# Chunk 0's value products moved from the start of its attention to its projection units, with its rows' affine passes

## What is computed

```
x    = layer_norm(x, emb_ln_g, emb_ln_b)
proj = x @ w_in          # u_pool 512 | q 512 | c 128 | iq 512 | ik 64 | iw 8
pool_out = per-group matmul of (trailing-window mean of u_pool - u_pool), windows 2,4,8,16
c    = rms_norm(c)       # the shared key/value latent
o    = sparse attention: scores from iq, ik, iw; causal top 256; softmax over c with bias
attn = o @ w_uv
x    = layer_norm(ALPHA*x + concat(pool_out, attn) @ w_o)
x    = layer_norm(ALPHA*x + square(relu(x @ w_up)) @ w_down)
```

## Time and profile before

| | |
|---|---|
| median of 3 runs | 1262.57 us (1261.06 to 1264.2) |
| the profiled execution, its own time | 1262.74 us |
| its span in the profile | 1261.0 us |
| PE busy | 1196.6 us (95%) |
| DVE, ACT, POOL busy | 867.2, 540.3, 518.0 us |
| mean granted TensorE clock | 0.987 |

### The profile page before, as it was taken

One profiled execution on the slowest core, in us unless ns is written; L12 is line 12 of the kernel. 1 busy time (PEld: TensorE's weight loads), 2 busy tenths in 40 slices (PEclk: granted clock), 3 DMA queues, 4 the chain that ended last, 5 costly groups with the idle time before them and its releaser, 6 DMA issues.

```text
span 1261.0 us, 16226 instructions
## 1 busy us (share of the span) xinstructions
PE 1196.6 (95%) x5551; PEld 962.9 (76%) x5551; DVE 867.2 (69%) x1291; ACT 540.3 (43%) x875; POOL 518.0 (41%) x396
## 2 busy tenths in 40 slices
PE   5999997789989999999999999979899999999997
PEld 4776785567888878778778768868788888888886
DVE  6388989686957888898998878867534233243357
ACT  4545542565246334334234266652342442433440
POOL 2235788433435676676676653212102102103002
PEclk9999899899999999999999999999999999999999
DMA  7723431101303233233333210035122333323331
GB/s 221 251 75 109 142 100 51 67 2 34 101 27 124 84 117 110 91 116 100 99 103 114 62 56 1 2 134 134 66 100 86 109 97 95 116 85 98 116 101 67
DMA packets 126852, 118.63 MB, mean 94 GB/s; under 512 B 5773, under 2 KB 99530, under 8 KB 126794
## 3 DMA queue, kind: packets, MB, share of 16 engines
q1 hardware_dynamic: 126794, 117.86, 30.4%
HBM read 107.34 MB, written 10.50 MB: 93 GB/s over the span
## 4 chain that ended last, share of the span: by engine, by line
PE 76%; DVE 9%; POOL 7%; issue 3%; ACT 2%; DMA 2%; POOLq 0%; DVEq 0%; SPq 0%; ACTq 0%
PE g_bank L1641 14%; PE g_bank L1642 14%; PE g_bank L1643 14%; PE wide L1641 8%; PE wide L1643 8%; PE wide L1642 8%; PE g_bank L1799 3%; POOL wlo L453 3%; PE g_bank L1601 2%; POOL rows L858 1%; DVE win L628 1%; PE wide L1758 1%; PE wide L1705 1%; PE wide L1706 1%; POOL rstd L779 1%
## 5 line engine op out<-in xcount | busy, mean ns | idle before, releaser
L453 POOL TENSOR_TENSOR wlo<-wring,whi 128x1024 fp32r<-128x1024 f32 (+1 forms) x94 | 229.8, 2446 | 204.4 <-ACT whi L1505 123.4
L1641 PE MATMUL g_bank<-xhi,whi 128*128 128x512 f32 (+2 forms) x768 | 301.4, 392 | 4.3 <-DVE xlo L694 3.9
L1642 PE MATMUL g_bank<-xlo,whi 128*128 128x512 f32 (+2 forms) x768 | 297.7, 388 | 0.0
L1643 PE MATMUL g_bank<-xhi,wlo 128*128 128x512 f32 (+2 forms) x768 | 297.6, 388 | 0.0
L1505 ACT ACTIVATE whi<-wring 128x1024 fp32r<-128x1024 f32 x120 | 127.1, 1059 | 355.9 <-PE wide L1643 179.8
L453 DVE TENSOR_TENSOR wlo<-wring,whi 128x1024 fp32r<-128x1024 f32 (+1 forms) x66 | 84.4, 1278 | 197.8 <-ACT whi L1505 192.8
L1641 PE MATMUL wide<-whi,hhi 128*128 128x512 f32 x480 | 190.2, 396 | 0.7 <-POOL wlo L453 0.7
L1643 PE MATMUL wide<-whi,hlo 128*128 128x512 f32 x480 | 189.6, 395 | 0.0
L1642 PE MATMUL wide<-wlo,hhi 128*128 128x512 f32 x480 | 189.6, 395 | 0.0
L1641 PEld LDWEIGHTS g_bank<-xhi,whi 128*128 128x128 f32 (+1 forms) x768 | 144.6, 188 | 39.7 <-DVE xlo L694 4.3
L1643 PEld LDWEIGHTS g_bank<-xhi,wlo 128*128 128x128 f32 (+1 forms) x768 | 144.6, 188 | 33.0 <-issue 0.6
(11 more groups left out here) (238 smaller groups left out, 1953.4 us busy)
## 6 DMA issues: line engine op xcount, KB each, us to landing
wring<-in_w_up SPq DMA_DIRECT2D x64, 512.0 KB, 4.1
wring<-in_w_down SPq DMA_DIRECT2D x64, 512.0 KB, 3.7
wring<-in_w_in SPq DMA_DIRECT2D x26, 512.0 KB, 3.9
wring<-in_w_o SPq DMA_DIRECT2D x16, 512.0 KB, 4.1
rows<-in_x SPq DMA_DIRECT2D x8, 512.0 KB, 4.9
normalized_rows<-rows SPq DMA_DIRECT2D x8, 512.0 KB, 6.9
rows<-normalized_rows SPq DMA_DIRECT2D x4, 512.0 KB, 5.1
emb_stage<-normalized_rows SPq DMA_DIRECT2D x4, 512.0 KB, 4.6
```

The costliest lines, as they stand in the source:

```text
L453: eng.tensor_tensor(parts_of(name, lo_tile(name)), parts_of(name, wring[n % 4]), parts_of(name, hi_tile(name)).bitcast(F32), ALU.subtract) ...
L1641: nc.tensor.matmul(out_ap, w_hi, m_hi, start=first, stop=False)
L1642: nc.tensor.matmul(out_ap, w_hi, m_lo, start=False, stop=False)
L1643: return nc.tensor.matmul(out_ap, w_lo, m_hi, start=False, stop=last)
```

## The change

Chunk 0's values are formed among its own projection units: `("vv", 0, k)` enters the order of `tokens_queries(0)`, PE and ACT form it there, and DVE's low parts go into its loop over n. The latents of chunk 0 are rounded right after they are made, into tiles of their own (`latT0_hi`, `latT0_lo`), and their low part is made before the poolings. Values 2 and 3 use the tiles at 104.25 and 108.25 KB, where `gains` lies; so ACT waits before each value for the four blocks of `emb_gains`, and SP waits for the last value product of the attention (`pv_full`, 16) before it loads the next gains. `emb_gains` now works on the rows before they are spilled: POOL starts it once iq unit 1 is split, and does its eight passes, the latents' inverse (`latents_inverse_rms`) and the subtraction for `wuv_lo` among its first splits. The rows that come back from the spill area need nothing more. `head_masks` waits for unit q3 of chunk 1 and no longer for po3.

```diff
-    order = ("u0 u1 u2 po0 u3 po1 q0 po2 q1 po3 q2 q3", "q0 q1 q2 u0 u1 u2 po0 u3 po1 q3 po2 po3")[c]
+    order = ("u0 u1 vv0 u2 vv1 po0 u3 vv2 po1 q0 vv3 po2 q1 po3 q2 q3", "q0 q1 q2 u0 u1 u2 po0 u3 po1 q3 po2 po3")[c]
...
-        names += [("vv", c, k) for k in ((0, 1, 2, 3), (2, 3, 4, 5, 6, 7))[c]]
+        names += [("vv", 1, k) for k in range(2, NB)] if c else []
...
+LAST_UNIT = ("q", 1, 3)
...
+        latT0_hi = part("latT0_hi", 84.25, [P, CHUNK], F32R)
+        latT0_lo = part("latT0_lo", 86.25, [P, CHUNK], F32R)
...
+            tile = v_part[k] if c == 0 and k >= 2 else v_tiles[k]
...
-            load_units(units[4:7])
-
+            load_units(units[4:8])
+
+            sp.wait_ge(bias_row_ready, 1)
+            sp.dma_start(bias_rows, bias_row[:, :]).then_inc(bias_out, 16)
             for b in range(CB):
-                sp.wait_ge(xhat_ready, b + 1)
+                load_units(units[8 + b:9 + b])
+                if b == 1:
+                    sp.wait_ge(bias_out, 16)
+                    sp.wait_ge(wuv_lo_ready, 1)
+                    sp.dma_start(near_up[:, :, :], ...).then_inc(bias_in, 16)
+                sp.wait_ge(emb_rows, b + 1)
                 sp.dma_start(spilld[b], rows[:, b, :]).then_inc(spilled, 16)
             sp.wait_ge(spilled, 16 * CB)
-
-            sp.wait_ge(g_full, EV[("xT", 0, KT - 1)])
             for b in range(CB):
                 sp.dma_start(rows[:, b, :], xd[CB + b]).then_inc(x_in[CB + b], 16)
-
-            sp.wait_ge(bias_row_ready, 1)
-            ...
-            load_units(units[7:U[("iq", 1, 3)]])
+            load_units(units[12:U[("iq", 1, 3)]])
...
-            sp.wait_ge(emb_rows, CB)
+            sp.wait_ge(pv_full, 16)
             load_gains(ln1_g, ln1_b)
...
-                pool.wait_ge(g_full, EV[("po", 1, 3)])
+                pool.wait_ge(g_full, EV[LAST_UNIT])
...
-            def emb_gains():
+            def emb_gains(b):
 
                 pool.wait_ge(gains_in, 32)
-                for b in range(CB):
-                    pool.wait_ge(rows_in, 16 * (b + 1))
-                    ...
+                pool.wait_ge(g_full, EV[("xT", 0, KT - 1)])
+                link(pool.tensor_tensor(rows[:, b, :], rows[:, b, :], gains[:, 0, :], ALU.mult))
+                pool.tensor_tensor(rows[:, b, :], rows[:, b, :], gains[:, 1, :], ALU.add).then_inc(emb_rows, 1)
...
             inverse_std(EMB0)
+
+            pool.wait_ge(*LO[("iq", 0, 1)])
+            emb_gains(0)
+            emb_gains(1)
+            latents_inverse_rms(0)
             pool.wait_ge(wuv_hi_ready, 1)
             pool.tensor_tensor(wuv_lo[:, :], wuv_raw[:, :], wuv_hi[:, :].bitcast(F32), ALU.subtract).then_inc(wuv_lo_ready, 1)
-            latents_inverse_rms(0)
-            lo(*units[U[("u", 0, 0)]:U[("q", 0, 2)]])
+            emb_gains(2)
+            lo(("u", 0, 0))
+            emb_gains(3)
+            lo(*units[U[("u", 0, 0)] + 1:U[("q", 0, 2)]])
...
-            gained = emb_gains()
-            for name in units[U[("iq", 1, 3)] + 3:U[("wo", 0, 0, 2)]]:
-                lo(name)
-                next(gained)
+            lo(*units[U[("iq", 1, 3)] + 3:U[("wo", 0, 0, 2)]])
             head_masks(0)
...
             keys_queries_lo(dve, 0, chain, lambda p: split_lo(dve, dve_lo[3 + p], lo_dve) if p < 3 else None)
+            latents_lo(0)
...
                 add_score(2 * n + 1)
+                if 1 <= n <= 4:
+                    values_lo(0, n - 1)
...
-            latents_lo(0)
             attention(0)
...
                 copy_out(("cT", c), latT[:, c * CHUNK:(c + 1) * CHUNK], bank(("cT", c))[:, :], scale=kv_g)
+                if c == 0:
+                    act.wait_ge(g_evac, EV[("cT", 0)])
+                    nc.scalar.activation(latT0_hi[:, :], latT[:, 0:CHUNK], ACT.Copy).then_inc(latT_hi_ready, 1)
...
+                    if name[0] == "vv":
+                        act.wait_ge(emb_rows, CB)
+                        values_hi(0, n)
+                        continue
...
-            act.wait_ge(iq_lo_ready, 2 * CB)
-            nc.scalar.activation(latT_hi[:, 0:CHUNK], latT[:, 0:CHUNK], ACT.Copy).then_inc(latT_hi_ready, 1)
             attention(0)
...
+                    if name[0] == "vv":
+                        values(0, name[2])
+                        continue
...
-                for k in ((0, 1, 2, 3), (2, 3, 4, 5, 6, 7))[c]:
-                    values(c, k)
+                for k in range(2, NB) if c else ():
+                    values(1, k)
```

More of the change, by code:

```diff
@@ L270, in layer, with v_pairs @@
         v_tiles = v_keep + v_part + [whi[1]]
-        def v_pairs(k):
-            return v_tiles[k][:, :].rearrange("p (a b d) -> p a b d", a=4, b=4)
+        def v_pairs(c, k):
+            tile = v_part[k] if c == 0 and k >= 2 else v_tiles[k]
+            return tile[:, :].rearrange("p (a b d) -> p a b d", a=4, b=4)
         def halves(v):
@@ L388, in layer @@
             units += [("ik", c), ("c", c)] + [("iq", c, p) for p in range(4)]
-            units += [name for name in tokens_queries(c) if name[0] != "po"]
+            units += [name for name in tokens_queries(c) if name[0] in ("u", "q")]
         for c in range(2):
@@ L832, in head_masks @@
                 spread_reciprocals(8 * c + 7)
-            def emb_gains():
+            def emb_gains(b):
                 pool.wait_ge(gains_in, 32)
-                for b in range(CB):
-                    pool.wait_ge(rows_in, 16 * (b + 1))
-                    link(pool.tensor_tensor(rows[:, b, :], rows[:, b, :], gains[:, 0, :], ALU.mult))
-                    yield b
-                    pool.tensor_tensor(rows[:, b, :], rows[:, b, :], gains[:, 1, :], ALU.add).then_inc(emb_rows, 1)
-                    yield b
+                pool.wait_ge(g_full, EV[("xT", 0, KT - 1)])
+                link(pool.tensor_tensor(rows[:, b, :], rows[:, b, :], gains[:, 0, :], ALU.mult))
+                pool.tensor_tensor(rows[:, b, :], rows[:, b, :], gains[:, 1, :], ALU.add).then_inc(emb_rows, 1)
             def staged_gains(b):
@@ L1080, in latents_lo @@
                 at = slice(0, CHUNK * (c + 1))
+                hi_part, lo_part = ((latT0_hi, latT0_lo), (latT_hi, latT_lo))[c]
                 dve.wait_ge(latT_hi_ready, c + 1)
-                nc.vector.tensor_tensor(latT_lo[:, at], latT[:, at], latT_hi[:, at].bitcast(F32), ALU.subtract)\
+                nc.vector.tensor_tensor(lo_part[:, :], latT[:, at], hi_part[:, :].bitcast(F32), ALU.subtract)\
                     .then_inc(latT_lo_ready, 1)
@@ L1126, in attention @@
                         mask_logits(step)
-                    if step == 32 * c:
-                        for k in ((0, 1, 2, 3), (2, 3, 4, 5, 6, 7))[c]:
-                            values_lo(c, k)
+                    if c and step == 32:
+                        for k in range(2, NB):
+                            values_lo(1, k)
                     if 32 * c + 2 <= step < 32 * c + 34:
@@ L1165, in add_residual @@
                 dve.wait_ge(rows_in, 16 * CB * (c + 1))
-                dve.wait_ge(emb_rows, CB * (c + 1))
+                if c:
+                    dve.wait_ge(emb_rows, 2 * CB)
                 for nh, u, b in projection_steps():
@@ L1423, in attention @@
                 exps(lo)
-                for k in ((0, 1, 2, 3), (2, 3, 4, 5, 6, 7))[c]:
-                    values_hi(c, k)
+                for k in range(2, NB) if c else ():
+                    values_hi(1, k)
                 for step in range(lo, lo + LAST_STEP):
@@ L1742, in values @@
                 free(name)
-                three_passes(bank(name)[:, :], latT_hi[:, at], latT_lo[:, at], wuv_hi[:, :], wuv_lo[:, :], True, True)\
+                three_passes(bank(name)[:, :], hi_part[:, at], lo_part[:, at], wuv_hi[:, :], wuv_lo[:, :], True, True)\
                     .then_inc(g_full, 1)
```

14 lines of the change are left out of this document (6 added, 8 removed).

## The result

The changed kernel takes **1256.14 us** (median of 6 runs, 1253.44 to 1258.6) where the kernel before takes 1262.42 (6 runs beside them, 1261.06 to 1264.2). The ratio is 0.9948 with a 95% interval of 0.9933 to 0.9963: 6.3 us faster. The profiled execution of the changed kernel took 1258.6 us (span 1256.8), 4.1 less than the profiled one of before. It is the slowest of the six; the granted clock of the six is between 0.990 and 0.996, and the two fastest runs, 1253.44 and 1255.12 us, have the highest, 0.996 and 0.995.

A forecast was written before the change was run, and what follows sets the result against it. PE was taken to bind until 113 us, and DVE's poolings, in turns with POOL, from 189.63. -13.4 + 2.8 + 1.1 + 6.4 = -3.1 against 1262.74 gave 1259.6, so 1259.5 us as median; range 1252.5 to 1265.

The forecast's parts named there:

- rival A: Among the iq units, POOL and DVE operations fit each other's gaps, so Part 3 is 0: 1253.1 us; chance 0.22.
- Part 3: Among the iq units, POOL's added passes delay DVE's splits: PE waits 1.3 and 3.5 us, low clock 1.6; loss 6.4 us.
- Part 2: In chunk 0's u and q units, four values cost PE 2.8 us and waits at po1 and po2 1.1.
- `values_lo` would be the releaser: In chunk 0's units, waits before po1 and po2 stay below 1 us and end with `values_lo`.
- Part 1: End of chunk 1's projections and attention's start: earlier poolings and values moved away bring the fourth logits forward; gain 13.4 us.
- Rival D: At the attention's start, masks wait for something other than the last split; about 8 us gained, 1265 us; 0.18 with B.
- 1.2 us for a low clock: At the attention's new start, PE idles between 214.6 and 218 us and the clock falls; 1.2 us (0 to 2.5) given back.
- the wait before po1: End of chunk 1's projections: po1's 0.67 us wait for pooled group 1 goes, moving everything to q3 forward by 0.67.
- The edits costed at nothing: Chunk 0's latent rounding, ACT's wait for `emb_rows`, later spills and loads, and SP's later w_o load have slack; 0 us.
- Rivals B and C: B: DVE falls behind in chunk 0's units, 1261 to 1265 us, 0.18 with D. C: turns continue, 1266.8 us, 0.10.
- the two stretches that I placed: Low clock after PE idles: 1.6 us lost among the iq units and 1.2 us at the attention's new start.

The follow-up runs named there:

- e1: Changed kernel without POOL's eight passes over chunk 0's rows, all waits kept; 1251.86 us, ratio 0.9910 to the kernel before.
- e4: Changed kernel's work in another POOL order, keeping passes clear of DVE's subtractions and splits for iq units 2 and 3; 1251.61 us, ratio 0.9907.
- e5: Changed kernel with each block's two passes replaced by four memsets of the same rows, which read nothing; 1252.2 us (one run).
- e3: Changed kernel with values early, but eight same-size passes back behind POOL's last eight splits of chunk 1; 1260.05 us, ratio 0.9980.
- e6: Changed kernel with POOL's last split before the masks moved into the attention, ahead of mask 18; 1255.07 us, ratio 0.9938.
- e7: e4 with wuv_lo ahead of block 2's passes, these around u0's split, and block 3's passes together behind u1's split; 1257.76 us, ratio 0.9957.
- e2: Changed kernel with passes early, but chunk 0's values and latent rounding put back at the attention's start; 1255.84 us, ratio 0.9943.
- e9: e4 with wuv_lo right behind the first four passes and the last split late as in e6; 1248.9 us, ratio 0.9895.
- e10: e9 with the values late as in e2; 1250.33 us, ratio 0.9908 to the kernel before.

## Why the prediction was right, and where its sizes were off

The time lies in the range, 3.4 us under the predicted 1259.5. The gain is 6.3 us where 3.1 were forecast, and the result is 0.4 us below the forecast's own range (1256.5 to 1262.5), towards rival A, which did not happen. The kernel is faster by more than the noise, an outcome given 0.42 against 0.48 for no change. So the range held in part because it was wide enough for rival A. Each mechanism named was there; what was off is a sum of small terms and the clock.

- **Part 3, the turns among the iq units** (predicted +6.4). The step held: waits of 1.06 and 2.94 us for 1.3 and 3.5, starts at 47.31 and 56.12 for 47.6 and 56.7 to 57, a stretch at half clock right behind. u0 ended 5.68 us later. e1 and e4 take the loss away in two ways, e5 in a third that keeps POOL writing in the passes' place. With that rival A is out: the rule of exclusion decides, and not a sharing of bandwidth, which would have left this part near 0. The estimate was 0.7 high. The stage runs 0.27 earlier from its start (L718 at 42.49, L715 at 42.76 in rows 7). Counted from start to start, as the prediction counts, the two units came 1.22 and 3.17 us late (46.36 - 0.27 + 1.22 = 47.31, and 47.31 + 5.64 + 3.17 = 56.12), 0.4 less than the 4.8 predicted. That is 0.4 more than PE's idle time, since a product lasts 0.40 us where one starts every 0.23: the last one before a wait still runs to its end. What is left, 1.56 us, is the low clock, for which 1.6 was taken.
- **Part 2, the values among chunk 0's units** (predicted 2.8 + 1.1). Measured 4.13. The term of 0.235 us a pass was exact, as a value between its neighbours in the timeline of PE shows:

```profile
76.41 0.39 PE L1655 MATMUL g_bank<-wuv_hi,latT_hi 128*128 128x512 f32 x1
...
77.11 0.40 PE L1655 MATMUL g_bank<-xhi,whi 128*128 128x512 f32 x1
```

Four times 0.70 is 2.8. The waits make up the other 1.3, where 1.1 was predicted: PE idled 0.33 and 0.50 us (0.35 and 0.75 predicted), and as in part 3 the idle time is not all that they cost. po1 starts 1.19 us behind the first product of its value and po2 1.36, where 0.70 would do without a wait, and the unit behind each starts 0.08 us later than behind a po that did not wait. That `values_lo` would be the releaser holds for po2; at po1 ACT's copy came last, with `values_lo` at 91.65 to 92.33 just ahead of it.
- **Part 1, the gain** (predicted 13.4). The times of the last stage, put 9.25 us later for what lies ahead, are the predicted ones: the last split at 222.78 (213.5 + 9.25 = 222.75), the first memset at 225.20 (215.9 + 9.25 = 225.15), the masks at 226.38 (226.35), the fourth logits at 228.23 (228.05). e3 and e6 show that the chain is the right one: put the passes back and 6.3 of the 13.7 us are gone again, take the last split out and 2.6 more are won. Rival D, that the masks wait for something else, is out with it. Of the 1.2 us for a low clock only 0.52 showed, as a longer attention: the clock was at 0.82 over the 9.5 us from 221.5.
- **What was not in the sum**: 0.59 us in chunk 1 beyond the wait before po1. Before, the clock was low for longer around 126 us (0.66 over 124 to 134, where the changed kernel has 1.00 and then 0.57 over 138 to 142); the attribution is argued. And 0.47 us over the last 975, where nothing was changed. That stretch took between 972.2 and 975.7 us in the twelve profiled executions, so 0.47 says nothing. The edits costed at nothing cost nothing: ACT takes the w_o unit at 300.74 us, 4.66 earlier than before (305.40), like all that stands around it.
- **Rivals B and C** did not come. POOL's passes ended at 63.9 us and PE had no third wait at the iq units or u0, and DVE's slack among the units sufficed; e7 used it up with 6.4 us.
- **The point and the sign.** From profile to profile the sum was 1.1 us short: -0.7 (part 3), +0.2 (part 2), -0.6 (chunk 1), -1.0 (the start), +1.0 (the rest). The other 2.1 us of the 3.2 that the forecast missed lie between executions: before's profiled one is near its median, and the profiled one of the changed kernel was its slowest. One place where such a difference arises is on record, the low clock behind the idle PE of rows 10. The changed kernel's profiled execution has it too (0.73 over 347 to 353 us); in e2 and e9 the clock is 1.00 over the same instructions, and the stretch from the output projection on is some 3 us shorter. The term that was mis-sized is thus the low clock that would be left: the sum took it to stay as before, apart from the two stretches that I placed. The mean clock of the 40 runs of before beside the experiments was 0.984 to 0.990, that of the six runs after 0.990 to 0.996. Why the changed kernel is granted more in its usual execution stays open, as there is one profile of each.

## What to carry to other kernels

When work is moved away from a place that binds, look at both places and at what stands last at the old one; here 9.8 of 15.0 us went back at the new place, and an order of the same instructions that looked after both (e9) gained twice as much.

## What the runs showed of the hardware

- **The size of VectorE's operation does not matter for what it pays.** Operations on 1 and 16 columns took 2.25 to 2.33 us under POOL's 2.4 us operations (e7), 0.16 to 0.17 us without; a copy of 16 columns at the end of chunk 1 took 2.07 before and, in the changed kernel under a split, 2.00.
- **Memsets on GpSimd do not hold VectorE.** 0.69 us for L718 and L719 with a memset running beside them, where a pass made it 2.78 (e5).
- **The low parts of the values are not held.** `values_lo` has one input in PSUM and one in SBUF. In the changed kernel it took 0.68 us from 91.65 while POOL's split began at 91.97 and took 2.37; neither was longer than alone.
- **Where the clock falls is not the same for one program from run to run.** The changed kernel's six executions have a mean granted clock of 0.990 to 0.996 and times from 1258.6 to 1253.4 us, and e1, e4 and e10 have a low stretch from 22 us on in their profiled executions that the other nine lack, with the same instructions up to there. A difference of 2 us between two single profiles of this kernel is no finding.
